# Router matmuls with the router's columns stationary, token rows kept whole in f32, and the Fourier mixer's time transform in two halves

## The reference, cut to what matters

```python
ya = jnp.real(jnp.fft.fft2(a.astype(jnp.float32), axes=(1, 3), norm='ortho'))   # over 256 positions, 128 channels
...
logits = (h @ router_w).astype(jnp.float32)          # (256, 1024) @ (1024, 8)
top_v, top_i = lax.top_k(logits, TOP_K)
top_p = jax.nn.softmax(top_v, axis=-1)
...
for e in range(N_EXPERTS):
    y = y + comb[..., e:e + 1] * swiglu(h, w1[e], w3[e], w2[e])
```

## Time and profile before

| | us |
|---|---|
| median of 3 runs | 1850.13 |
| the three runs | 1850.13, 1851.99, 1847.75 |
| the profiled execution, its own time | 1844.99 |
| span of its trace | 1843.2 |
| busy in the span: PE / DVE / ACT | 1762.5 / 848.5 / 691.7 |

### The profile page before, as it was taken

How to read it: one execution, slowest core, us unless ns; L and a number is a source line. 1 busy time by engine, 2 the same in 40 slices (tenths; PEclk the granted TensorE clock), 3 DMA queues, 4 the chain that set the end, 5 groups by cost and what they waited for, 6 DMA issues and landing times.

```text
span 1843.2 us, 28265 instructions
## 1 busy us (share of the span) xinstructions
PE 1762.5 (96%) x11540; PEld 1305.3 (71%) x11540; DVE 848.5 (46%) x1195; ACT 691.7 (38%) x896; POOL 4.5 (0%) x6
## 2 busy tenths in 40 slices
PE   6999999999999999997999999999999999998987
PEld 3677677888887899997877877766546887653433
DVE  3434425434533656756569875554104555410111
ACT  4332622222224726534467655543003454400001
POOL 0000000000000000000000000000000000000000
PEclk9999999999999999998999999999999999999999
DMA  9835266434621331320279889999999999999996
GB/s 362 297 125 171 81 221 237 158 93 150 226 92 57 103 91 59 92 81 23 69 269 332 334 331 408 409 409 409 408 409 399 406 407 408 406 408 409 409 409 244
DMA packets 161843, 479.96 MB, mean 260 GB/s; under 512 B 14976, under 2 KB 58160, under 8 KB 155568
## 3 DMA queue, kind: packets, MB, share of 16 engines
q1 hardware_dynamic: 161712, 478.14, 68.5%
HBM read 477.03 MB, written 1.05 MB: 259 GB/s over the span
## 4 chain that ended last, share of the span: by engine, by line
PE 71%; DMA 17%; DVE 4%; ACT 3%; SPq 3%; issue 2%; DVEq 0%; ACTq 0%
PE ps L676 17%; PE ps L678 16%; PE ps L677 16%; DMA arena<-in_moe_up 5%; PE ps L1429 5%; DMA arena<-in_moe_w 4%; DMA raw<-in_moe_up 4%; DMA raw<-in_moe_w 3%; SPq L625 2%; DVE w_lo L1982 2%; PE ps L1500 2%; PE ps L695 1%; PE ps L1084 1%; PE ps L1418 1%; PE ps L1082 1%
## 5 line engine op out<-in xcount | busy, mean ns | idle before, releaser
L1982 DVE TENSOR_TENSOR w_lo<-raw,w_hi 128x1024 fp32r<-128x1024 f32 x242 | 292.6, 1221 | 317.3 <-ACT w_hi L1595 313.5
L1595 ACT ACTIVATE w_hi<-raw 128x1024 fp32r<-128x1024 f32 x242 | 253.3, 1056 | 422.0 <-PE ps L678 329.6
L676 PE MATMUL ps<-h_hi,w_hi 128*128 128x512 f32 (+1 forms) x736 | 279.2, 379 | 3.0 <-DVE h_lo L2064 2.2
L678 PE MATMUL ps<-h_lo,w_hi 128*128 128x512 f32 (+1 forms) x736 | 273.3, 371 | 0.0
L677 PE MATMUL ps<-h_hi,w_lo 128*128 128x512 f32 (+1 forms) x736 | 273.0, 371 | 0.0
L1982 DVE TENSOR_TENSOR w_lo<-arena,w_hi 128x1024 fp32r<-128x1024 f32 x144 | 174.0, 1223 | 100.3 <-ACT w_hi L1595 95.3
L1595 ACT ACTIVATE w_hi<-arena 128x1024 fp32r<-128x1024 f32 x144 | 152.4, 1060 | 126.3 <-DMA arena<-in_moe_up 65.3
L676 PEld LDWEIGHTS ps<-h_hi,w_hi 128*128 128x128 f32 x736 | 138.6, 188 | 47.4 <-issue 22.1
L678 PEld LDWEIGHTS ps<-h_lo,w_hi 128*128 128x128 f32 x736 | 138.6, 188 | 24.5
L677 PEld LDWEIGHTS ps<-h_hi,w_lo 128*128 128x128 f32 x736 | 138.8, 189 | 22.6 <-issue 0.5
L676 PE MATMUL ps<-w_hi,s_hi 128*128 128x512 f32 x336 | 134.1, 399 | 4.0 <-DVE w_lo L1982 3.3
(11 more groups left out here) (364 smaller groups left out, 2281.3 us busy)
## 6 DMA issues: line engine op xcount, KB each, us to landing
arena<-in_moe_up SPq DMA_DIRECT2D x256, 512.0 KB, 11.7
raw<-in_moe_up SPq DMA_DIRECT2D x192, 512.0 KB, 11.1
arena<-in_moe_w SPq DMA_DIRECT2D x128, 512.0 KB, 14.0
raw<-in_moe_w SPq DMA_DIRECT2D x96, 512.0 KB, 14.5
arena<-in_w_ada SPq DMA_DIRECT2D x35, 1024.0 KB, 5.0
raw<-in_ffn_w SPq DMA_DIRECT2D x66, 512.0 KB, 5.8
raw<-in_w_in_odd SPq DMA_DIRECT2D x40, 512.0 KB, 3.6
scratch<-in_w_ada SPq DMA_DIRECT2D x11, 1024.0 KB, 6.1
```

Of the source, the lines that this page charges most:

```text
L676: pe.matmul(dst, s_h, m_h, start=start, stop=False, **kw)
L678: return pe.matmul(dst, s_h, m_l, start=False, stop=stop, **kw)
L1595: act.activation(w_hi[:, o % R, :], src, ACT.Copy).then_inc(hi_done, 1)
L1982: dve.tensor_tensor(w_lo[:, o % R, :], src, w_hi[:, o % R, :].bitcast(F32), ALU.subtract).then_inc(lo_done, 1)
```

## The change

TensorE, time transform: the cosine matmuls write only columns 0 to 128 (129 of them) and the sine matmuls only columns 1 to 127 (127 of them), beside one another in the same bank; nothing is added up between the two. ScalarE copies the bank to `arena` (the place of `M_A`). VectorE makes columns 1 to 127 as sum, columns 255 down to 129 as difference, and copies columns 0 and 128; then come the hi and lo parts as for the gated heads.

```diff
+Y_EVEN, Y_ODD = N_LAT // 2 + 1, N_LAT // 2 - 1
...
-                        pe.matmul(ps[:, g, s * 256:(s + 1) * 256], acs[:, tok, g, 0:P],
-                                  ar(M_DFT + DFT_CT + t * N_LAT, N_LAT), start=(t == 0), stop=False)
-                        m = pe.matmul(ps[:, g, s * 256:(s + 1) * 256], acs[:, tok, g, P:2 * P],
-                                      ar(M_DFT + DFT_ST + t * N_LAT, N_LAT), start=False, stop=(t == LT - 1))
+                        tok, even, odd = s * LT + t, s * N_LAT, s * N_LAT + Y_EVEN
+                        pe.matmul(ps[:, g, even:even + Y_EVEN], acs[:, tok, g, 0:P],
+                                  ar(M_DFT + DFT_CT + t * N_LAT, Y_EVEN), start=(t == 0), stop=(t == LT - 1),
+                                  skip_group_check=True)
+                        m = pe.matmul(ps[:, g, odd:odd + Y_ODD], acs[:, tok, g, P:2 * P],
+                                      ar(M_DFT + DFT_ST + t * N_LAT + 1, Y_ODD), start=False, stop=(t == LT - 1),
+                                      skip_group_check=True)
...
-                    pe.wait_ge(y32_done, 1)
+                    pe.wait_ge(y32_done, 5)
...
+            def y_high(h):
+                act.wait_ge(y32_done, h + 1)
+                act.activation(hh(h), ar(M_TMP + h % 2 * NT, NT), ACT.Copy).then_inc(yhi_done, 1)
             for g in range(4):
                 act.wait_ge(y_mm, g + 1)
-                act.activation(hh(g), ps[:, g, :], ACT.Copy).then_inc(yhi_done, 1)
...
+                act.activation(ar(M_A + g * NT, NT), ps[:, g, :], ACT.Copy).then_inc(dft_out, 1)
+                if g:
+                    y_high(g - 1)
+            for h in range(3, 8):
+                y_high(h)
...
+            def y_low(g):
+                dve.wait_ge(yhi_done, g + 1)
+                dve.tensor_tensor(hl(g), ar(M_TMP + g % 2 * NT, NT), hh(g).bitcast(F32),
+                                  ALU.subtract).then_inc(ylo_done, 1)
+            def y_whole(g):
+                dve.wait_ge(dft_out, 8 + g + 1)
+                if g >= 2:
+                    dve.wait_ge(ylo_done, g - 1)
+                y = ar(M_TMP + g % 2 * NT, NT).rearrange("p (s t) -> p s t", s=2)
+                copy = ar(M_A + g * NT, NT).rearrange("p (s t) -> p s t", s=2)
+                even, odd = ps[:, g, :].rearrange("p (s t) -> p s t", s=2)[:, :, 1:Y_EVEN - 1], copy[:, :, Y_EVEN:]
+                dve.tensor_tensor(y[:, :, 1:Y_EVEN - 1], even, odd, ALU.add)
+                dve.tensor_tensor(y[:, :, Y_EVEN:][:, :, ::-1], even, odd, ALU.subtract)
+                dve.tensor_copy(y[:, :, 0:Y_EVEN:Y_EVEN - 1], copy[:, :, 0:Y_EVEN:Y_EVEN - 1]).then_inc(y32_done, 1)
             for g in range(4):
-                dve.wait_ge(yhi_done, g + 1)
-                dve.tensor_tensor(hl(g), ps[:, g, :], hh(g).bitcast(F32), ALU.subtract).then_inc(ylo_done, 1)
+                y_whole(g)
+                if g:
+                    y_low(g - 1)
+            y_low(3)
```

```diff
+        logits = scratch[0:N_EXP, 0:N_LAT]
+        eye = onehot[:, 0, :]
+        def tokens(t, kt, n=1):
+            return xT[:, kt:kt + n, N_LAT + t * P:N_LAT + (t + 1) * P]
...
+            def tokens_of(kt):
+                for t in range(LT):
+                    dst = ps[:, 4 + 2 * t + kt // 4, kt % 4 * P:(kt % 4 + 1) * P]
+                    pe.matmul(dst, hh(kt, t * P, (t + 1) * P), eye, start=True, stop=False)
+                    m = pe.matmul(dst, hl(kt, t * P, (t + 1) * P), eye, start=False, stop=True)
+                    if kt % 4 == 3:
+                        m.then_inc(tk_mm, 1)
...
             for kt in range(KT):
                 pe.wait_ge(h_done, 3 * KT + kt + 1)
-                for t in range(LT):
-                    m = three(ps[:, 2 * t, 0:N_EXP], hh(kt, t * P, (t + 1) * P), hl(kt, t * P, (t + 1) * P),
...
+                m = three(ps[0:N_EXP, 0, 0:N_LAT], rt_hi[:, kt * N_EXP:(kt + 1) * N_EXP],
+                          rt_lo[:, kt * N_EXP:(kt + 1) * N_EXP], hh(kt, 0, N_LAT), hl(kt, 0, N_LAT),
+                          kt == 0, kt == KT - 1)
+                if kt == KT - 1:
+                    m.then_inc(lg_mm, 1)
+                if kt:
+                    tokens_of(kt - 1)
+            tokens_of(KT - 1)
+            pe.wait_ge(lg_out, 1)
+            for t in range(LT):
+                m = pe.transpose(ps[:, 2, t * N_EXP:(t + 1) * N_EXP], logits[:, t * P:(t + 1) * P], ...)
             m.then_inc(lg_mm, 1)
-            for part in (h_hi, h_lo):     # 32 transposes, L1221
...
+            warm(3, 2)
+            pe.wait_ge(lg_out, 2)         # was: pick, 1
...
-                for q, part in enumerate((s_hi, s_lo)):
-                    for kt in range(KT):
+                for kt in range(KT):
+                    for t in range(LT):
+                        i = pe.matmul(ps[:, kt // 4, kt % 4 * P:(kt % 4 + 1) * P],
+                                      tokens(t, kt)[:, 0, :], onehot[:, t, :].bitcast(F32), ...)
+                    if kt % 4 == 3:
+                        i.then_inc(ga_mm, 1)
...
-            pe.wait_ge(tk_out, 8)
-            warm(4, 1)
+            pe.wait_ge(tk_out, 4)
+            warm(3, 1)
             gather_m(0)
-            warm(4, 2)
```

More of the change, by code:

```diff
@@ L1226, in _ @@
-            pe.wait_ge(pick, 1)
+                m = three(ps[0:N_EXP, 0, 0:N_LAT], rt_hi[:, kt * N_EXP:(kt + 1) * N_EXP],
[8 more added lines that the diff above has]
+            for t in range(LT):
+                m = pe.transpose(ps[:, 2, t * N_EXP:(t + 1) * N_EXP], logits[:, t * P:(t + 1) * P],
+                                 con[0:N_EXP, C_ID:C_ID + N_EXP])
@@ L1235, in gather_m @@
                 pe.wait_ge(oh_rdy, tally(m, 1, 1))
-                for q, part in enumerate((s_hi, s_lo)):
-                    for kt in range(KT):
[L1238 to L1242, removed]
+                for kt in range(KT):
+                    for t in range(LT):
+                        i = pe.matmul(ps[:, kt // 4, kt % 4 * P:(kt % 4 + 1) * P],
+                                      tokens(t, kt)[:, 0, :], onehot[:, t, :].bitcast(F32),
+                                      start=(t == 0), stop=(t == LT - 1))
+                    if kt % 4 == 3:
+                        i.then_inc(ga_mm, 1)
             def gather_s(s, bank):
@@ L1247, in gather_s @@
                 for kt in range(KT):
[L1248 to L1251, removed]
-                                          start=(q == 0 and t == 0), stop=(q == 1 and t == LT - 1))
+                    for t in range(LT):
+                        i = pe.matmul(ps[:, bank, kt * HALF:(kt + 1) * HALF],
+                                      tokens(t, kt)[:, 0, :],
+                                      onehot_s[:, t, 0:HALF].bitcast(F32), start=(t == 0), stop=(t == LT - 1))
                 i.then_inc(sx_ga, 1)
@@ L1396, in moe_turn @@
                             for k in range(4):
+                                if v == 0 and k == 2:
+                                    pe.wait_ge(ga_lo, 2 * m + 2)
                                 hi, lo = m_unit(v + k)
@@ L1690, in _ @@
                                ACT.Copy).then_inc(dft_out, 1)
+            def y_high(h):
+                act.wait_ge(y32_done, h + 1)
+                act.activation(hh(h), ar(M_TMP + h % 2 * NT, NT), ACT.Copy).then_inc(yhi_done, 1)
             for g in range(4):
                 act.wait_ge(y_mm, g + 1)
-                act.activation(hh(g), ps[:, g, :], ACT.Copy).then_inc(yhi_done, 1)
-            for h in range(4):
-                act.wait_ge(y32_done, h + 1)
-                act.activation(hh(4 + h), ar(M_TMP + h % 2 * NT, NT), ACT.Copy).then_inc(yhi_done, 1)
+                act.activation(ar(M_A + g * NT, NT), ps[:, g, :], ACT.Copy).then_inc(dft_out, 1)
[3 more added lines that the diff above has]
+                y_high(h)
             split_to(U_FFN + LEAD - 1)
@@ L2374, in _ @@
             dve.wait_ge(lg_mm, 1)
-            for t in range(LT):
-                m = dve.tensor_copy(route[:, t, 0:8], ps[:, 2 * t, 0:N_EXP])
-            link(m)
+            dve.tensor_copy(logits, ps[0:N_EXP, 0, 0:N_LAT]).then_inc(lg_out, 1)
+            dve.wait_ge(lg_mm, 2)
+            link(dve.tensor_copy(route[:, :, 0:8], ps[:, 2, 0:LT * N_EXP].rearrange("p (t e) -> p t e", t=LT)))
             for t in range(LT):
@@ L2501, in gather_lo @@
             def gather_lo(m):
-                dve.wait_ge(ga_hi, tally(m, 1, 1))
-                dve.tensor_copy(s_lo[:, 2048:3072], ps[:, 2:4, :]).then_inc(ga_lo, 1)
+                for half in range(2):
+                    part = slice(2048 + half * BANK, 2048 + (half + 1) * BANK)
+                    dve.wait_ge(ga_hi, tally(m, 2, half + 1))
+                    dve.tensor_tensor(s_lo[:, part], ps[:, half, :], s_hi[:, part].bitcast(F32),
+                                      ALU.subtract).then_inc(ga_lo, 1)
             def one_hots(col):
@@ L2532, in one_hots_q @@
                 i.then_inc(sx_oh, 1)
+            dve.wait_ge(tk_mm, 4)
```

45 lines of the change are left out of this document (15 added, 30 removed).

## The result

The changed kernel took 1832.74 us (median of four executions, 1831.51 to 1832.87) against 1851.06 of the kernel before in the same comparison (1847.75 to 1853.35): a ratio of 0.9901, 95% interval 0.9889 to 0.9914. It is faster by 18.3 us; forecast were 13.9 and 1836.2. Its profiled execution took 1832.75, its span is 1830.9.

A forecast was written before the change was run, and what follows sets the result against it. TensorE was taken to carry 71% of the chain of waits, DMA 17%, with DMA full from about 1090 us. Terms 6.6 + 5.8 + 1.5 = 13.9 us, off the median 1850.1, gave 1836.2; range 1833 to 1844.

The forecast's parts named there:

- A: Whole kernel: the three gains add up to 13.9 us, own range 1834 to 1838; chance 0.47.
- B to F: Five rivals: router clock falls 0.20, VectorE splits 0.10, lasting half clock 0.05, weight stream 0.10, extra loop pass 0.02.
- The transform: Time transform: 64 instructions go from 0.216 to 0.112 us each, evacuation covered; term 6.6 us.
- The router and first gather: Router's first product to first expert product: ranks no longer wait behind transposes, copies leave the chain; gain 5.8 us.
- The end of the first turn: Gathers ending the first expert turn: the clock stays up for the eight products behind them; 1.5 us, ends 0 and 1.7.
- C: First expert turn: VectorE's splits set its pace, so 4.0 us counts and not 5.8, giving 1838.0; chance 0.10.
- Later gathers: Gathers after the first turn: covered by the DMA, gain 0.
- the weight stream: Weight DMA: full only from about 1090 us, so TensorE time saved before that comes off the end.
- E: After 930 us: the weight stream sets everything, only the transform's 6.6 us is left, 1843.5; chance 0.10.
- The low end: Lower end of the forecast range: 1833 us, not put nearer because the runs before lie 4 us apart.
- Rival B: Router: the clock falls as before, at 930.7 for 6.9 us; gain 3.5 and not 5.8, 1838.5; chance 0.20.

The follow-up runs named there:

- experiment 9: Kernel before with only the router's columns made stationary (24 products of 256 columns, two small transposes), token transposes and float32r gathers kept: 1844.59 us, ratio 0.9963.
- experiment 3: Kernel before with the router and gathers part of the change alone, transform as before: 1840.63 us, ratio 0.9937.
- experiments 2: Kernel before with the time transform's part of the change and nothing else: 1845.12 us, ratio 0.9957.
- experiments 5: Changed kernel with its router products turned back to 48 of 8 moving columns, identity products and gathers kept: 1843.58 us, ratio 0.9960.
- experiment 8: Kernel before with its 32 transposes replaced by float32r products with the identity, 8-column router products kept: 1860.29 us, ratio 1.0054.
- experiment 6: Changed kernel with the 64-column gathers back in float32r from rounded token rows, in two passes: 1834.79 us, ratio 0.9911.

## Why the prediction was wrong

**The mechanism held, the base did not.** The likeliest case, A, is what happened: faster, clock full through the router, no case of B to F. The range missed the median by 0.3 us, the sum missed the gain by 4.4. In the pair of traces on which it can be tried, the three terms measured 6.7, 5.9 and 1.6, in all 14.2 where 13.9 were forecast.

- **The transform**, 6.6: 6.66 in the trace. VectorE's operations took 0.42, 0.41, 0.16 and 0.69, the reversed write (L2175) no more than the plain one, so its end of 1.2 falls away. The cover is 0.7 us and not 0.5.
- **The router and first gather**, 5.8: 5.94 against the same trace as the sum, 21.33 - 15.39. The ranks started 927.94 - 919.16 = 8.8 us after the first product, forecast 9.1; the first expert product came 15.4 after it, forecast 15.6. Against a second execution of the kernel before the gain is 7.84, since that one lost the clock twice.
- **The end of the first turn**, 1.5: 1.6. From the start of the two gathers to the end of the eight products it was 10.57 us and is 8.99, and 10.52 in the second execution of before. The size is right. The clock does stay up, but by experiment 9 the f32 gathers are not shown to be the reason. These two places gain 9.4 against the second execution, near the 10 to 11 of experiment 3.
- **C** isn't paid: from the first expert product to the start of the gathers it takes 99.4 us after the change and 99.7 before, with VectorE's splits in both chains.
- **Later gathers**, 0, and **the weight stream**: both parts' gains reached the end (experiments 2 and 3), and E is out. Behind the eight products the changed kernel's trace is 2.1 us longer than the first of before and 0.6 shorter than the second, so a small loss there can't be told from scatter.

**The step that failed** is the last one of the sum: "Taken off the median of 1850.1, 1836.2". It subtracts a difference worked out in one execution, which lay 5.1 us under the median, from the median. That supposes that the changed kernel's executions also scatter 5 us above such a trace. They don't: its profiled execution took 1832.75 and its median is 1832.74. Against the trace used, the gain was 12.3 us, 1.6 less than the sum, though the terms gave 14.2: the trace was lucky up to the transform (1.4 us shorter than the changed kernel's), behind the eight products (2.1 shorter), and in its clock (0.990 where 57 others have 0.982 to 0.989). In its router stage the kernel before has half clock for 7 us in one execution and, in two falls, for 14 in another; the changed kernel has none there in its three traces, and experiments 5 and 9 show that the 8-column products are what the first fall follows. So the change gains more against the mean execution than against the mild one. The second trace is 6.9 us longer than the first: 3.2 up to the transform, 1.9 in the router stage, 2.7 behind the eight products, 0.5 in the first turn, and 1.4 less in the heads. Shown are the two traces, the clocks of the 57 executions and experiments 5 and 9. That the clock makes 4.3 us of difference is worked out from a line through scattered points. How much of the offset the clock makes outside the router, and what makes the difference ahead of the transform, isn't settled.

**The low end.** The text allowed "1 us of runs' scatter" downward and ended the range at 1833 since "the runs before lie 4 us apart". A known distance of 5.1 us between trace and median was a reason to end it near 1831, which the sum itself named for the successor of that execution. Such a range would have held the result by its width, without the right centre.

**Rival B**, the clock falling in the router as before, did not come: it is 1.00 there in the three traces of the changed kernel. The 32 transposes did not hold it low: the clock fell before the first and rose before the last, stayed up through all 32 in experiment 9, and did not rise when float32r products stood in their place (experiment 8). The float32r pairs of weight load and product took 3.50 / 32 = 0.109 in experiment 6, as in the earlier trace rows. The Trainium skill's 81 ns for such a pair (TensorE: Matmul & The Clock Gate, Back-to-back issue gap) is met nowhere here.

## What to carry to other kernels

Before a sum from one trace is taken off a median, compare that execution's own time and mean granted clock with those of the others: where its clock lies above theirs and its time below, a change that removes what the clock is lost to gains more than the trace shows. In a chain of waits, look up the first instruction of a stage in the timeline as well: here the chain left out the router's first block, 0.63 us. Products that move 8 columns over 128x128 weights cost far more than their own time here (11 us for 48 of them); make the narrow operand the stationary one. Where TensorE's chain waits in pieces, seven dummy products inside the waits bought another 3 to 6 us of 1833 in three versions out of four; in the fourth, five more at the end outlasted their wait, and it gained nothing.

## What I had not expected of the hardware

- At half clock, a stream of float32r weight loads and products of 128 columns, busy all the time, left the clock at half for 23.8 us; with transposes in place of 32 of them it rose after 6.8.
- The same instructions around the same idle 1.65 us left the clock up in two of four executions and down in two.
- Float32r gathers of 64 columns were followed by half clock in five traces and by full clock in a sixth.
- A vector write in reversed order ran at 413 ns, the plain one of the same size at 422.
